# A transformer and DeltaNet layer on one core: adaLN columns and two gate columns as narrow products, x loaded first

## The reference

```
mod = silu(c) @ w_ada + b_ada            # c: 1024 values, w_ada: 1024 x 6144
sh1, sc1, gt1, sh2, sc2, gt2 = split(mod)
h    = rmsnorm(x, norm1_g) * (1 + sc1) + sh1
proj = h @ w_in                          # 1024 x 5640: attention q, k, v; q, k, v, z of
                                         # the DeltaNet; its a and b (8 columns); two gates
```

## Time and profile before

| | us |
|---|---|
| median of 3 runs | 1651.31 |
| lowest, highest | 1647.70, 1651.38 |
| profiled execution | 1652.54 |
| its span | 1649.9 |
| PE, DVE, ACT, POOL busy | 1608.8, 927.8, 638.9, 266.0 |

### The profile page before, as it was taken

The page is one execution under the profiler, slowest core; times in us unless marked ns, Lnnn a source line. Parts: engine busy times, 40 slices in busy tenths (PEclk is TensorE's granted clock), DMA queues, the critical chain, the costliest instruction groups (busy, mean ns, idle before and its releaser), DMA issues.

```text
span 1649.9 us, 24004 instructions
## 1 busy us (share of the span) xinstructions
PE 1608.8 (98%) x8235; PEld 1328.9 (81%) x8235; DVE 927.8 (56%) x1459; ACT 638.9 (39%) x1308; POOL 266.0 (16%) x283
## 2 busy tenths in 40 slices
PE   5999999999999999999899999999999999999998
PEld 5877878888878787878788877888888888888887
DVE  5867665445444444545553399866666666334424
ACT  4234456555534444444212235333333333332413
POOL 1016580111110101100000012322332220000000
PEclk9999999999999999999999999999999999999999
DMA  9835657655833333422546312222222223643412
GB/s 296 221 104 191 223 170 227 183 178 153 250 101 106 103 108 97 132 101 99 171 148 203 102 53 77 97 84 87 76 76 76 95 75 138 216 177 130 145 45 102
DMA packets 223652, 223.42 MB, mean 135 GB/s; under 512 B 18025, under 2 KB 189162, under 8 KB 223594
## 3 DMA queue, kind: packets, MB, share of 16 engines
q1 hardware_dynamic: 216618, 197.50, 38.0%
q0 software_dynamic: 6976, 25.17, 4.0%
HBM read 162.35 MB, written 60.29 MB: 135 GB/s over the span
## 4 chain that ended last, share of the span: by engine, by line
PE 81%; DVE 4%; DMA 1%; ACT 1%; issue 0%; DVEq 0%; SPq 0%; ACTq 0%
PE pm L1595 22%; PE pm L1609 15%; PE pd L1454 11%; PE ps L1194 11%; PE pm L1194 9%; PE sc L1407 2%; PE tT L1430 2%; PE tT L1419 2%; PE pm L1507 1%; PE gps L1344 1%; DMA gst<-z_d 1%; PE pm L1549 1%; PE gps L1357 1%; PE gps L1378 1%; PE gps L1371 1%; PE gps L1364 1%
## 5 line engine op out<-in xcount | busy, mean ns | idle before, releaser
L1194 PE MATMUL ps<-act_hi,w_hi 128*128 128x512 f32 x464 | 154.4, 414 | 5.3 <-DVE est L2273 2.8
L2167 DVE TENSOR_TENSOR w_lo<-w_raw,w_hi 128x1024 fp32r<-128x1024 f32 x61 | 78.6, 1289 | 125.1 <-ACT w_hi L1701 115.6
L1194 PE MATMUL ps<-act_lo,w_hi 128*128 128x512 f32 x464 | 143.7, 391 | 0.0
L1194 PE MATMUL ps<-act_hi,w_lo 128*128 128x512 f32 x464 | 143.4, 390 | 0.0
L1609 PE MATMUL pm<-act_hi,w_hi 128*128 128x512 f32 x352 | 137.2, 390 | 0.0
L1609 PE MATMUL pm<-act_hi,w_lo 128*128 128x512 f32 x352 | 137.0, 389 | 0.0
L1609 PE MATMUL pm<-act_lo,w_hi 128*128 128x512 f32 x352 | 136.9, 389 | 0.0
L1595 PE MATMUL pm<-act_hi,w_hi 128*128 128x512 f32 x320 | 124.5, 389 | 0.0
L1595 PE MATMUL pm<-act_lo,w_hi 128*128 128x512 f32 x320 | 124.5, 389 | 0.0
L1595 PE MATMUL pm<-act_hi,w_lo 128*128 128x512 f32 x320 | 124.5, 389 | 0.0
L1454 PE MATMUL pd<-act_hi,w_hi 128*128 128x512 f32 x256 | 111.3, 435 | 0.0
(11 more groups left out here) (367 smaller groups left out, 3452.4 us busy)
## 6 DMA issues: line engine op xcount, KB each, us to landing
w_raw<-in_w_in_dram SPq DMA_DIRECT2D x45, 512.0 KB, 5.6
w_raw<-in_w_ffn_in_dram SPq DMA_DIRECT2D x44, 512.0 KB, 3.7
h_raw<-h_d SPq DMA_DIRECT2D x36, 512.0 KB, 3.4
a_raw<-in_w_ada_dram SPq DMA_DIRECT2D x32, 512.0 KB, 4.5
w_raw<-in_w_ffn_out_dram SPq DMA_DIRECT2D x44, 256.0 KB, 3.7
h_d<-hid SPq DMA_DIRECT2D x21, 512.0 KB, 2.6
pk_d<-pk SPq DMA_DIRECT2D x8, 768.0 KB, 3.7
qkva_d<-est POOLq DMA_DIRECT2D x12, 512.0 KB, 6.3
```

The costliest lines, as they stand in the source:

```text
L1194: ins = pe.matmul(dst[:, cols], wt[:, ds % 2, k, :], at[:, cols], start=(first and n == 0), stop=(last and n == 2))
L2167: dve.tensor_tensor(w_lo[:, ds % 2], w_raw[:, ds % NR], w_hi[:, ds % 2].bitcast(F32), ALU.subtract)\
```

## The change

- SP: x goes ahead of the first part of w_ada. Unit 0 is no longer loaded as 128 columns; 32 columns of w_in (8 of use) go to wab. The three small loads stay behind the second part of w_ada; wab counts on the same semaphore (misc_in) as two of them.
- PE: `columns(n)` multiplies all eight rows of a part with silu(c) as 32 equal stationary columns and the part's 512 columns moving, k % 4 choosing the 32 output partitions of aT. ACT copies aT to asum (`copy_columns`), and `turn_columns(n)` adds the four groups and puts the columns on partitions: 4 products of 128 columns. DVE's `ada_sum` is gone. The columns of part 0 come behind the broadcast.
- PE: unit 0 becomes four blocks of 8 fp32 products of 512 frames with 32 stationary columns (`ab_block`, one for every two k), each of hi and lo of each k in its own group of 32 output partitions of ps0. The groups are added where a and b are turned, with sel, which is 1 where p % 32 == h, in place of the identity. POOL makes sel.
- ACT and DVE: the split of unit 0 is gone, that of unit 1 is made before the first pair's norms. ACT's copies of columns stand ahead of act_hi 0, 3 and 5.

```diff
@@ in the allocations
+        sel = sb("sel", [P, 2 * B_H])
...
+            wab = sbin(st0, "wab", [P, KT, 32])
@@ sync
-            load_ada(0)
             for t in range(NT):
                 load_x(t)
+            load_ada(0)
+            sp.dma_start(wab[:, :, :], w_in_v[:, :, C_AB:C_AB + AB_COLS]).then_inc(misc_in, 16)
+            sp.sem_inc(raw_in[0], 16)
+            load_unit(1, 0, w_in_v, C_QKVB + group(1) * P)
             load_ada(1)
-            for d in range(2):
-                load_unit(d, 0, w_in_v, C_AB if d == 0 else C_QKVB + group(1) * P)
@@ gpsimd
+            pool.wait_ge(consts_ready, 3)
+            ch.link(pool.tensor_tensor(sel[:, :], ident[:, 0:8], ident[:, AB_COLS:AB_COLS + 8], ALU.add))
+            ch.link(pool.tensor_tensor(sel[:, :], sel[:, :], ident[:, 2 * AB_COLS:2 * AB_COLS + 8], ALU.add))
+            pool.tensor_tensor(sel[:, :], sel[:, :], ident[:, 3 * AB_COLS:3 * AB_COLS + 8], ALU.add)\
+                .then_inc(consts_ready, 1)
@@ tensor
-            def units01(n):
-                for d, k in in_step(2 * n, 2 * n + 2):
...
+            def ab_block(k):
+                if k == 1:
+                    pe.wait_ge(misc_in, 48)
+                for b in (k - 1, k):
+                    for x, at in enumerate((act_hi, act_lo)):
+                        for h in range(2):
+                            c = 2 * b + x
+                            rows = slice(c % 4 * AB_COLS, (c % 4 + 1) * AB_COLS)
+                            ins = pe.matmul(ps[0][rows, half(h)], wab[:, b, :], at[:, b, half(h)].bitcast(F32),
+                                            start=(c < 4), stop=(c >= 2 * KT - 4))
+                if k == KT - 1:
+                    ins.then_inc(dense_mm, 1)
+
+            def units01(k):
+                pe.wait_ge(lo_ready, k + 1)
+                if k % 2:
+                    ab_block(k)
+                ins = dense_k(1, k, ps[1], act_hi[:, k, :], act_lo[:, k, :], k == 0, k == KT - 1)
...
+            def columns(n):
+                pe.wait_ge(ada_in[n], ada_count(n))
+                if n:
+                    pe.wait_ge(asum_ready, n)
+                for k in range(KT):
+                    ins = pe.matmul(aT[k % 4 * AB_COLS:(k % 4 + 1) * AB_COLS, :],
+                                    cs[:, k:k + 1].broadcast_to([P, AB_COLS]), ada_row(n, k),
+                                    start=(k < 4), stop=(k >= 4))
+                ins.then_inc(mod_mm, 1)
+
+            def turn_columns(n):
+                pe.wait_ge(asum_ready, n + 1)
+                if n:
+                    pe.wait_ge(mod_ready, n)
+                for q in range(4):
+                    ins = pe.matmul(gps[:, q * P:(q + 1) * P], asum[:, n % 2, q * P:(q + 1) * P],
+                                    sel[:, 0:1].broadcast_to([P, P]), start=True, stop=True)
+                ins.then_inc(mod_mm, 1)
...
-            modulation(0)
-            beat(12)
+            beat(8)
             pe.wait_ge(diag_ready, 1)
...
-            modulation(1)
+            pe.wait_ge(cs_ready, 1)
+            columns(0)
+            pe.wait_ge(vecT_ready, 2)
+            pe.wait_ge(consts_ready, 4)
+            turn_columns(0)
+            columns(1)
+            turn_columns(1)
+            pe.wait_ge(xt_read, NT)
             beat(8)
-            pe.wait_ge(xt_read, NT)
             pe.wait_ge(wlo_ready, 2)
             units01(0)
-            modulation(2)
+            columns(2)
             units01(1)
-            modulation(3)
+            turn_columns(2)
             units01(2)
             units01(3)
+            columns(3)
+            units01(4)
+            turn_columns(3)
+            for k in (5, 6, 7):
+                units01(k)
...
-                        ins = pe.transpose(gps[:, t * 8:(t + 1) * 8], est[0:8, 0, t * P:(t + 1) * P],
-                                           ident[0:8, 0:8])
+                        ins = pe.matmul(gps[:, t * 8:(t + 1) * 8], est[:, 0, t * P:(t + 1) * P], sel[:, :],
+                                        start=True, stop=True)
@@ scalar
+            def copy_columns(n):
+                act.wait_ge(mod_mm, 2 * n + 1)
+                act.activation(asum[:, n % 2, :], aT[:, :], ACT.Copy).then_inc(asum_ready, 1)
...
-            act.wait_ge(misc_in, 32)
+            act.sem_inc(whi_ready, 1)
+            split_hi(1)
+            act.wait_ge(misc_in, 48)
             act.activation(negA[:, :], negA[:, :], ACT.Exp).then_inc(act_chain, 1)
-            for n in range(4):
-                for k in (2 * n, 2 * n + 1):
...
-                    if n == 0:
-                        split_hi(k)
+            copy_columns(0)
+            copy_columns(1)
+            for k in range(KT):
+                if k == 3:
+                    copy_columns(2)
+                if k == 5:
+                    copy_columns(3)
+...
-                    act.activation(est[0:8, 0, :], ps[0][0:8, :], ACT.Copy).then_inc(ab_read, 1)
+                    act.wait_ge(dense_mm, 1)
+                    act.activation(est[:, 0, :], ps[0][:, :], ACT.Copy).then_inc(ab_read, 1)
@@ vector
-            def ada_sum(n):
...
-            ada_sum(0)
...
             dve.wait_ge(xt_read, NT)
-            ada_sum(1)
+            dve.wait_ge(whi_ready, 1)
+            dve.sem_inc(wlo_ready, 1)
+            split_lo(1)
...
-                dve.wait_ge(mod_mm, n + 1)
+                dve.wait_ge(mod_mm, 2 * n + 2)
...
-                if n == 0:
-                    split_lo(0)
-                    split_lo(1)
```

More of the change, by code:

```diff
@@ L552, in hybrid_layer @@
         ACT_X = (3, 6)
+        AB_COLS = 32
         def ada_count(n):
@@ L1227, in _, with beat @@
             pe.transpose(gps[:, 0:n], vrow[:, :], ident[0:n, 0:n]).then_inc(vecT_mm, 1)
+            def columns(n):
[15 more added lines that the diff above has]
+                ins.then_inc(mod_mm, 1)
+            def beat(count):
+                for _ in range(count):
+                    pe.matmul(aT[:, 0:P], ones[:, :], ident[:, :], start=True, stop=True)
             for t in range(NT):
@@ L1236, in _ @@
                 ins.then_inc(xt_mm, 1)
-            def modulation(n):
-                pe.wait_ge(ada_in[n], ada_count(n))
-                pe.wait_ge(asum_ready, n + 1)
-                if n:
-                    pe.wait_ge(mod_ready, n)
-                for q in range(4):
-                    dst = gps[:, q * P:(q + 1) * P]
-                    for k in range(5, KT):
-                        pe.matmul(dst, ada_row(n, k)[:, q * P:(q + 1) * P], cs[:, k:k + 1].broadcast_to([P, P]),
-                                  start=(k == 5), stop=False)
-                    ins = pe.matmul(dst, asum[:, n % 2, q * P:(q + 1) * P], ones[:, :], start=False, stop=True)
-                ins.then_inc(mod_mm, 1)
-            def beat(count):
-                for _ in range(count):
-                    pe.matmul(aT[:, 0:P], ones[:, :], ident[:, :], start=True, stop=True)
-            pe.wait_ge(cs_ready, 1)
-            pe.wait_ge(vecT_ready, 2)
-            modulation(0)
-            beat(12)
+            beat(8)
             pe.wait_ge(diag_ready, 1)
@@ L1719, in _ @@
                                    ACT.Copy).then_inc(xt_read, 1)
-            act.wait_ge(misc_in, 32)
+            act.sem_inc(whi_ready, 1)
+            split_hi(1)
+            act.wait_ge(misc_in, 48)
             act.activation(negA[:, :], negA[:, :], ACT.Exp).then_inc(act_chain, 1)
-            for n in range(4):
-                for k in (2 * n, 2 * n + 1):
-                    act.wait_ge(xn_ready, k + 1)
-                    act.activation(act_hi[:, k, :], est[:, k % 2, :], ACT.Identity,
-                                   bias=modT[:, SH1 + k:SH1 + k + 1]).then_inc(hi_ready, 1)
-                    if n == 0:
-                        split_hi(k)
+            copy_columns(0)
[5 more added lines that the diff above has]
+                    copy_columns(3)
+                act.wait_ge(xn_ready, k + 1)
+                act.activation(act_hi[:, k, :], est[:, k % 2, :], ACT.Identity,
+                               bias=modT[:, SH1 + k:SH1 + k + 1]).then_inc(hi_ready, 1)
             def pre_decay(t):
```

22 lines of the change are left out of this document (5 added, 17 removed).

## The result

The change makes the kernel slower: 1663.62 us (median of 4 runs, 1661.78 to 1664.94) against 1651.17 (median of 4, 1647.70 to 1651.38), a ratio of 1.0074 with a 95% interval of 1.0062 to 1.0086. The forecast was 1649.4 with a range up to 1660.5. So the time lies outside the range, and on the other side of no change.

A forecast was written before the change was run, and what follows sets the result against it. TensorE, busy 98% of the span, was taken as the bound. First dense step 0.3 us earlier and 1.6 us won from there to unit 3 gave -1.9: 1651.3 to 1649.4 us, range 1645 to 1660.5.

The forecast's parts named there:

- (3): First dense step to unit 3: 39.0 us, narrow blocks 2.05 each; unit 3 at 82.2, 1.9 us earlier, kept to the end.
- (4): POOL's additions for sel, the earlier split of unit 1 and unit 2's wait for ab_read: at no cost.
- (1): Loads at the start: last x at 19.4, broadcast ends 27.4, dtb at 34.0; the early x gains nothing.
- (2): From the loads to the first dense step: at 43.2, 0.3 us earlier, with 1.7 us for a slow clock.
- Rival (e): PE's clock does not fall in the gap before 35 us: -3.6 us; shares the forecast's chance of 0.42.
- (a): Unit 0's narrow blocks: products of one group hinder each other, 3.8 us a block, +4.2 against before; chance 0.2.
- (b): Narrow products: at most two groups run at once, so columns cost 3.8 us too; +9.4, 1660.7; chance 0.15.
- (c): Narrow products: strict order, each group starting behind the last pass of the one before, 5.9 us a block; +17.5; chance 0.07.
- Rival (d): Start: loads come earlier still, dtb and w_ada's second part by 2 us; first step at 39.5, -5.5, 1646; chance 0.16.

The follow-up runs named there:

- + scale late: run 7 with ScalarE's scaling of a w_ada block moved behind the copy of the recurrence's product that shares its place; 1648.82 us, ratio 0.9986.
- + negA late: run 7 with ACT's exponential of negA, and its wait for small loads, moved behind the third act_hi; 1650.81 us, ratio 0.9995.
- + both: run 7 with both the exponential of negA behind the third act_hi and the later scaling of w_ada's block; 1649.89 us, ratio 0.9994.
- experiment 1: The kernel before with one unused tile of 32 bytes a partition where the change puts sel, nothing else; 1665.02 us, ratio 1.0077.
- 6: The kernel before with 256 unused bytes a partition ahead of t_hi; 1650.92 us, ratio 0.9990.
- run 7: The changed kernel with sel allocated at the end of the first stage's tiles, so later tiles lie where they lay before; 1650.75 us, ratio 1.0000.
- experiment 8: run 7 with the load order alone undone: the first part of w_ada ahead of x again; 1649.94 us, ratio 0.9997.
- experiment 5: A separate kernel of products alone, moving rows at 6 offsets by weight rows at 12; 228 ns or less where both share a place, multiple of 32, in 256 bytes.

## Why the prediction was wrong

How far each trace was ahead of before (us, by the start of the same instruction; one profiled execution each):

```
                            after  sel at end  + scale late  + negA late  + both
first dense step  (43.52)   -1.0      0.0         -0.2          +0.6       +2.8
unit 3            (84.14)   +0.5     +1.4         +1.3          +2.1       +4.3
gm by after      (120.16)   +1.1     +1.3         +0.9          +0.5       +0.8
turning of Um    (246.16)   +1.6     +1.6         +1.1          +1.5       +1.1
Tm by Ct         (249.74)   +0.2     +0.2         +1.3          +0.9       +1.4
last of y        (866.50)   -1.9      0.0         +2.8          +0.7       +1.8
final transposes (1620.77) -11.3     +0.3         +3.0          +0.9       +2.1
```

**The step that failed** is the last sentence of (3): "From there the order of work is the old one and PE is its bound (98%), so the 1.9 us should stay." It took the same work in the same order to mean the same time. What a product costs changed by 3% (226.7 to 233.3 ns), for those whose rows had moved relative to each other. Part (4), "POOL's three small additions for sel" at no cost, priced the instructions that write `sel` and not the place that it takes. The missing term is +12 to 13 us (12.8 in experiment 1; 1.0074 against 1.0000 between the change and run 7, 12.2), and experiments 1, 6 and 7 show it from three sides: a gap alone brings it, a gap of 256 bytes does not, and moving `sel` takes it away. No rival of the prediction had it. Its 12.2 us and the 1.9 that were forecast and did not last add up to 14.1; the measured time lies 14.2 above the forecast.

**The same sentence fails a second time**, as run 7 shows: a lead of 1.6 us at 246 is 0.2 at 249.5. PE is busy 98% of the span, but at single places it is held by transfers whose landing hardly moves. At 246 the scaling of w_ada's block had been the last thing ahead of Tm in before too; it only fitted there without a gap on PE. In the changed kernel it is PE's wait:

```profile
249.54 1.15 PE L1396 MATMUL gps<-Tm,Ct 128*128 128x128 f32 x8 [1.47 <-ACT Tm L1855]
```

A second place is at 96 to 106 us. A unit's evacuation into est waits until the store of two units before has landed. The first of these stores is issued at 82.56 in before and lands 15.0 us later; with both edits of 9 and 10 it is issued at 77.24 and takes 19.3. ACT of before, and ACT and PE of the run with both edits:

```profile
97.69 1.12 ACT L1776 ACTIVATE est<-ps,wcT 128x1024 f32<-128x1024 f32 x1 [5.21 <-DMA qkvb_d<-est]
```

```profile
96.69 1.11 ACT L1825 ACTIVATE est<-ps,wcT 128x1024 f32<-128x1024 f32 x1 [8.43 <-DMA qkvb_d<-est]
...
106.33 1.19 PE L1203 MATMUL ps<-act_hi,w_hi 128*128 128x512 f32 x2 [4.43 <-DVE est L2308]
```

Unit 3 started 4.3 us early in that run, and PE gave 4.43 back at 106.33. In all seven changed versions (first step between 44.97 and 40.68) this product starts between 106.08 and 106.52. What delays the store I did not try.

A third place is the wait for y_lo near 791 us. Run 7 starts behind it 1.04 us ahead of before, and by 798 is 0.05 ahead: it runs at granted clock 0.50 for 5.3 us, before for 3.2. In the run with the scaling late it is 3.2 too, and its lead stays, 2.76 at the wait and 2.8 at the last of y. So about 1 us of the leads of 0.3 and 3.0 at the end of the table hangs on when the clock came back in one execution, which the change does not set.

**The steps before that**, one by one:

- (1) Loads. First and last x at 6.58 and 19.62 (6.8 and 19.4 forecast). The broadcast was to end at 27.4; it starts at 26.53 and takes 3.44 us instead of 1.95, at granted clock 0.57, behind 2.60 us of idle. The forecast had no fall of the clock there. It ends at 30.0, and the wait for dtb hides that. "The early x is thus worth nothing" is right in the sum, and experiment 8 shows it; the way there was not only the wait for dtb. dtb came at 35.9, not 34.0: its order ahead cost 1.0 us more than before where I took 0.9 less.

```profile
35.93 0.20 ACT L1767 ACTIVATE negA<-negA 128x4 f32<-128x4 f32 x1 [6.74 <-DMA dtb<-in_dt_bias_dram]
36.04 0.58 ACT L1751 ACTIVATE asum<-aT 128x512 f32<-128x512 f32 x1
```

- (2) The first step at 44.54 instead of 43.2. Of the 1.3 us, 1.9 came from dtb, and the rest of the chain ran 0.6 shorter. Rival (e) falls, the clock does drop. Here is the stretch of after from 37 to 40 us, with the busy us and records of PE, PEld, DVE, ACT and POOL, then granted clock, DMA share and GB/s:

```profile
37.00:40.00 3.00, 3.00 (x16) 1.89 (x20) 1.08 (x3) 0.00 (x0) 0.00 (x0) 0.55 1.07 343
```

The granted clock is 0.55 there, near the lower of the two levels (1.2 GHz), behind 4.95 us of idle; 8 records of the turning take 2.05 us at it and 1.16 at 41.84.

- (3) Narrow blocks: forecast 2.05, measured about 1.9 from 47.85 to 49.72. This decides against rivals (a), (b) and (c).

```profile
47.85 0.59 PE L1234 MATMUL ps<-act_hi,wab 128*32 128x512 f32 x1
47.86 0.62 PE L1234 MATMUL ps<-act_lo,wab 128*32 128x512 f32 x1
47.87 0.62 PE L1234 MATMUL ps<-act_hi,wab 128*32 128x512 f32 x1
47.88 0.62 PE L1234 MATMUL ps<-act_lo,wab 128*32 128x512 f32 x1
48.28 0.59 PE L1234 MATMUL ps<-act_hi,wab 128*32 128x512 f32 x1
...
49.72 0.50 PE L1203 MATMUL ps<-act_hi,w_hi 128*128 128x512 f32 x1
```

The code issues the two halves of a group one behind the other, four records of one group, and still four groups start within 0.03 us, then the next record of each 0.43 later. So a later group starts ahead of an earlier group's remaining records. The Trainium skill (TensorE: Matmul & The Clock Gate, Part 3: Packing small matmuls) has matmuls start and end strictly in program order; the starts in these rows disagree. From the first dense step to unit 3 the forecast was 39.0 us and the trace has 39.1, with both waits for act_lo (0.60 and 0.55 for 0.9 and 0.7).

- Rival (d), loads earlier by 2 us, fell with dtb's landing. The part of the sum that I had worked out, -1.9 at unit 3, came out at -0.5, and at -1.4 in run 7, whose start is the same code: dtb came at 34.67 there. The difference of 0.9 us is that of one execution from another.

## What to carry to other kernels

When the same instructions run slower, count them per stretch at full clock and busy share: that tells a slower product from a wait. A tile added ahead of others can change the speed of everything behind it; put it last, or fill it up to 256 bytes, and keep moving rows and weight rows at the same place in 256 bytes and that place at a multiple of 32. This was measured for fp32r products of 128x128 by 128x512 alone. A lead won at the start lasts only to the next wait for a transfer, so look in the trace of before for every place where a load or a store ends the idle time of an engine that PE needs, and price the gain only up to the first of them. A wait behind which the clock is granted at 0.50 is such a place too: here it took 1 us of a lead.

## What the runs showed of the hardware

- A product of 128x128 by 128x512 in fp32r takes 226.7 ns from start to start, or up to 236.7 (experiment 5), by nothing but where its two operands' rows begin; with no other engine at work. Over a kernel of 1651 us a shift of 32 bytes came to 12.8 (experiment 1).
- The Trainium skill (SBUF — State Buffer, Operand start alignment) asks of an fp32 operand only a multiple of 4 bytes and says that this is about legality, not speed. Here every case was legal. The same page (A bandwidth-pool intuition that's wrong) gives weight loads a second, independent read port; that the time depends on how the two rows lie to each other (233.1 ns at 0 and 32, 226.9 at 32 and 32) is not what one would expect of it. Why it does, the runs do not show.
- Four column groups of fp32 products run beside each other, even when each has four records in a row: 16 records of 512 columns in about 1.9 us, where four records of one group alone stand 0.43 us apart.
- After the same wait near 791 us PE was back at granted clock 1.00 after 3.2 us of work in before and after 6.0 in after and 5.3 in run 7. A lead of 1 us can be lost there, or kept, without a difference in the code.
